# Experts' loop: low halves of the down weights made on GpSimd, those of gate and up on VectorE

## The chip, the cores and the metric

The kernel runs on one core of a Trainium2 chip. The metric is the device time of one execution, in microseconds (us). A core has five instruction streams that meet only at semaphores: TensorE (PE, matmuls; PEld is its weight load), VectorE (DVE), ScalarE (ACT), GpSimd (POOL) and SyncE (SP, which here only issues DMAs). Of these GpSimd also issues the indirect DMAs, the gathers and scatters by a list of row numbers.

## What is computed

The reference is two transformer-like blocks over 1024 tokens of width 1024. The change touches the expert layer, which is computed twice (once in each layer of the second block). Each of 16 experts takes its 128 best tokens, and adds its result to their rows:

```python
def ec_moe(h, w_router, w_gate, w_up, w_down):
    cap = EC_FACTOR * s // N_EXPERTS                 # 128 tokens for each of 16 experts
    aff = jax.nn.softmax(logits, axis=-1)
    gates, idx = lax.top_k(aff.transpose(0, 2, 1), cap)
    xs = jax.vmap(lambda hb, ib: hb[ib])(h, idx)     # gather
    g = jnp.einsum('becd,edf->becf', xs, w_gate)
    u = jnp.einsum('becd,edf->becf', xs, w_up)
    y = jnp.einsum('becf,efd->becd', jax.nn.silu(g) * u, w_down)
    y = y * gates[..., None].astype(y.dtype)
    ...                                              # scatter with add
```

## The kernel before

**Three passes.** A float32 product is made of reduced-precision parts. Each weight matrix `w` is split into a high part (a copy in the reduced type `fp32r`) and a low part (`w` minus the high part), and `three_passes` multiplies high by high, high by low, low by high. So for every weight slot two passes over 128 x 4096 elements are made ahead of the matmuls: the high part by ScalarE (`cast`, L3014) and the low part by VectorE (`low`, L3083). Both inputs of the low pass lie in SBUF.

**The weight ring.** All weights come in slots of 2 MB, through a ring of four buffers (`ring`). SyncE issues the load of slot n+4 when ScalarE has released slot n (L128 waits for L110). Each expert has three slots: gate, up and down. The order in the list is gate 0, up 0, gate 1, up 1, down 0, gate 2, up 2, down 1 and so on, so the down weights of expert e are slot 3e+4. The low part is written over the slot itself (`ring_r` is the same memory under the reduced type), the high part into one of four areas (named `oN_r` and `hT_r` in the trace).

**The loop.** Each engine runs its own loop over the experts, written as turns of four (`per_turn`). I write G, U and D for the gate, up and down products of an expert; each of G, U and D is 24 matmuls of 512 columns. In the iteration of expert j the engines do:

- TensorE: G of j+1, four transposes of the next expert's tokens (`turn_x`), four of the activation `a` (L2992), U of j+1, four more of `turn_x`, then D of j in two halves. D waits for the low part of the down weights.
- ScalarE: cast of slot 3j+4 (down), `gate` (release, SiLU), a copy of the tokens' high part, a copy of a's high part, cast of 3j+5 (gate), release of up, tokens again, cast of 3j+6 (up), and then the two halves of y (L3073), scaled out of PSUM; the second releases the down slot.
- VectorE: low of 3j+4 (down), `low_x` (L3134), low part of a (L3160), low of 3j+5 (gate), `gated` (L3140, silu(g) times u), `low_x`, low of 3j+6 (up).
- GpSimd: when y of e is in SBUF it runs a tiny add that takes the wait (`moe_taker`, 128 x 1, L2901), issues the scatter of e (L2920), runs another taker, and issues the gather of expert e+4 (L2911). Then it waits for the scatter's landing and raises `y_gone`, for which ScalarE waits before it overwrites that y buffer two experts later.

Semaphore `w_split` counts all low parts in the order of the slots; TensorE waits for its count ahead of each product.

Of the kernel before, what the change touches and what calls it, by code (L numbers as in the profile page):

```python
# [6 lines left out]
F32 = mybir.dt.float32  # L7
# [14 lines left out]
RING = 4  # L22
# [346 lines left out]
def start(eng, *sems):  # L369

    for s in sems:
        eng.nop().then_inc(s, 2)
# [2470 lines left out]
def moe_stage(nc, m, layer):  # L2843


    with Stage(nc, f"moe{layer}") as st:
        NE, CAP, EJ, K4 = 16, P, 4, 4
        TURNS = NE // EJ
        first = m["ring"].take(3 * NE)
# [13 lines left out]
        buf, buf_r = m["ring"].buf, m["ring"].buf_r  # L2863
        w_high = [m[t_][:, h_ * NT // 2:(h_ + 1) * NT // 2, :].rearrange("p t n -> p (t n)")
                  for t_ in ("oN_r", "hT_r") for h_ in range(2)]
# [2 lines left out]
        TP, AP_ = st.ps("xt_ps", [P, 4, P]), st.ps("at_ps", [P, 4, P])  # L2868
        G, U, Y = st.ps("g_ps", [P, 2, HALF]), st.ps("u_ps", [P, 2, HALF]), st.ps("y_ps", [P, 2, HALF])
        (wr_in, logits, lt_in, lt_turned, shifted, exped, aff_in, aff_T, work_in, topped, sel_T, sel_in, stepped,  # L2870
         xt_done, xt_cast, xt_in, w_cast, w_split, g_done, u_done, gu_free, sg_in, a_in, at_done, at_cast, at_in,
         y_done, y_in,
         added, y_gone) = (
            st.sem(x) for x in (
                "wr_in", "logits", "lt_in", "lt_turned", "shifted", "exped", "aff_in", "aff_T", "work_in", "topped", "sel_T", "sel_in",
                "stepped", "xt_done", "xt_cast", "xt_in", "w_cast", "w_split", "g_done", "u_done",
                "gu_free", "sg_in", "a_in", "at_done", "at_cast", "at_in", "y_done", "y_in", "added", "y_gone"))
        xs_in = [st.sem(f"xs_in{b}") for b in range(EJ)]
        block = st.block()
# [3 lines left out]
        SLOTS = 3 * EJ  # L2883

        def w_views(n, k):

            high, low = w_high[n % RING], buf_r[:, (first + n) % RING, :]
            return [v.rearrange("p (k n) -> p k n", k=k) for v in (high, low)]
# [6 lines left out]
        @block.gpsimd  # L2895
        def _(pool):
            pool.wait_ge(sel_in, 1)

            def take_wait(n):

                pool.tensor_tensor(taker[:, n:n + 1], zero[:], zero[:], ALU.add)  # L2901

            pool.memset(zero[:], 0.0).then_inc(zeroed, 1)
            pool.wait_ge(zeroed, 1)

            def gather(e):

                if e >= EJ:
                    pool.wait_ge(xt_in, 2 * (e - EJ + 1) + 1)
                take_wait(e)  # L2910
                pool.indirect_dma_start(xs[:, e % EJ, :], None, m["h"], bass.IndirectOffsetOnAxis(ap=rows[:, e:e + 1], axis=0))\  # L2911
                    .then_inc(xs_in[e % EJ], 16)

            start(pool, y_gone)
            for e in range(EJ):
                gather(e)
            for e in range(NE):
                pool.wait_ge(y_in, 2 * (e + 1) + 2)
                take_wait(NE + e)
                pool.indirect_dma_start(m["x1"], bass.IndirectOffsetOnAxis(ap=rows[:, e:e + 1], axis=0), y[:, e % 2, :],  # L2920
                                        None, compute_op=ALU.add).then_inc(added, 16)
                if e + EJ < NE:
                    gather(e + EJ)
                pool.wait_ge(added, 16 * (e + 1))
                pool.nop().then_inc(y_gone, 1)

        @block.tensor
        def _(pe):
# [32 lines left out]

            def product(i, j, what, done, n):

                pe.wait_ge(w_split, i * SLOTS + n + 1)
                if what is G:
                    pe.wait_ge(xt_in, i * (2 * EJ) + 2 * (j + 1) + 1)
                    pe.wait_ge(gu_free, i * EJ + (j + 1))
                w = w_views(n, KD)
                for k in range(KD):
                    ins = three_passes(pe, what[:, j % 2, :], [x_[:, j % 2, k, :] for x_ in (x_high, x_low)],  # L2970
                                       [w_[:, k, :] for w_ in w], k == 0, k == KD - 1)
                ins.then_inc(done, 1)
# [8 lines left out]
            def body(i, more):  # L2981

                for j in range(EJ):
                    nxt, after = more or j + 1 < EJ, more or j + 2 < EJ
                    if nxt:
                        product(i, j + 1, G, g_done, 3 * j + 2)
                    if after:
                        turn_x(i, j + 2, 0)
                    pe.wait_ge(a_in, i * EJ + (j + 1))
                    pe.wait_ge(at_in, i * EJ + (j + 1))  # L2990
                    for k in range(K4):
                        ins = pe.transpose(AP_[:, k, :], a[:, j % 2, k * P:(k + 1) * P], ids[:])  # L2992
                    ins.then_inc(at_done, 1)
                    if nxt:
                        product(i, j + 1, U, u_done, 3 * j + 3)
                    if after:
                        turn_x(i, j + 2, 1)
                    n = 3 * j + 4 if nxt else 3 * j + 2
                    w = w_views(n, K4)
                    pe.wait_ge(w_split, i * SLOTS + n + 1)  # L3000
                    pe.wait_ge(at_in, i * EJ + (j + 2))
                    for half in range(2):
                        pe.wait_ge(y_in, i * (2 * EJ) + 2 * j + half + 1)
                        for k in range(K4):
                            ins = three_passes(pe, Y[:, half, :], [a_[:, j % 2, k, :] for a_ in (a_high, a_low)],
                                               [w_[:, k, half * HALF:(half + 1) * HALF] for w_ in w], k == 0, k == K4 - 1)
                        ins.then_inc(y_done, 1)
# [70 lines left out]
        def _(dve):  # L3078
            step = Steps(dve, stepped)
            def low(i, n):  # L3080
                b = (first + n) % RING
                dve.wait_ge(w_cast, i * SLOTS + n + 1)
                dve.tensor_tensor(buf_r[:, b, :], buf[:, b, :], w_high[n % RING].bitcast(F32), ALU.subtract)\  # L3083
                   .then_inc(w_split, 1)
# [67 lines left out]
            def body(i, more):  # L3152
                for j in range(EJ):
                    nxt, after = more or j + 1 < EJ, more or j + 2 < EJ
                    if nxt:
                        low(i, 3 * j + 4)
                    if after:
                        low_x(i, j + 2, 0)
                    dve.wait_ge(at_cast, i * EJ + (j + 1))
                    dve.tensor_tensor(a_low[:, j % 2, :, :], AP_[:, :, :], a_high[:, j % 2, :, :].bitcast(F32), ALU.subtract)\  # L3160
                       .then_inc(at_in, 1)
                    if nxt:
                        low(i, 3 * j + 5)
                        gated(i, j + 1)
                    if after:
                        low_x(i, j + 2, 1)
                        low(i, 3 * j + 6)
# [219 lines left out]
```

## Time and profile before

| | us |
|---|---|
| three runs | 4507.63, 4508.22, 4508.64 |
| profiled execution, its own time | 4506.89 |
| its span | 4505.1 |
| TensorE busy | 3856.6 (86%) |
| VectorE busy | 2588.6 (57%) |
| GpSimd busy | 502.5 (11%) |
| first expert layer, taker of the first scatter to last write of y | 2934.27 to 3215.16 |
| second expert layer, taker of the first scatter to last write of y | 4186.53 to 4469.89 |

The profiled execution's time is 1.8 us over its span. Times in the rows are counted from the span's start. In a row of the timeline stand: start, duration, engine, line, operation, output and inputs, shapes; in brackets how long the engine was idle just before, and who released it. An instruction that is held back by another engine's use of memory does not show as idle: its row is longer. In a row of the windows stand, for each engine, busy time and number of instructions, then the clock that TensorE was granted (1.00 is 2.4 GHz, 0.50 is 1.2 GHz), the share of time in which the DMA engines were busy, and GB/s.

### The profile page before, as it was taken

What the parts mean: (1) busy time and instruction counts of PE and PEld (TensorE: products, weight loads), DVE (VectorE), ACT (ScalarE), POOL (GpSimd) and SP (SyncE); (2) the same over time, 40 slices, a digit from 0 to 9 for tenths busy, and PEclk for the clock granted to TensorE, in tenths of its full rate; (3) what the DMA queues carried; (4) which work ended last, traced back from release to release, by engine and by line L of the source; (5) the groups of instructions that cost most, each with busy time, mean ns of one, the idle gap of its engine ahead of it and who ended that gap; (6) DMA issues with size and microseconds to landing.
All of it is one profiled execution on the core that took longest, in us unless ns stands there. A gap on an engine that the chain in (4) does not pass through costs nothing. (4 is left out here: it accounts for less than half of the span.)

```text
span 4505.1 us, 56411 instructions
## 1 busy us (share of the span) xinstructions
PE 3856.6 (86%) x22256; PEld 3126.4 (69%) x22256; DVE 2588.6 (57%) x3973; ACT 1651.8 (37%) x2217; POOL 502.5 (11%) x471
## 2 busy tenths in 40 slices
PE   5988998977897999999797999499677798994996
PEld 2766876766676888886697887277566587872774
DVE  6266771159555555555433773587655465745776
ACT  2213331146330000003113773276613465732675
POOL 0001121000000000000131000034102000000341
PEclk9989999989898999999898999699888899996998
DMA  7101112230431111111213103299702302022998
GB/s 296 42 22 61 64 64 96 73 126 22 140 134 66 56 37 56 53 40 69 91 59 142 34 16 137 93 377 371 237 21 81 83 21 110 15 103 94 352 377 277
DMA packets 136489, 518.88 MB, mean 115 GB/s; under 512 B 17952, under 2 KB 70336, under 8 KB 118224
## 3 DMA queue, kind: packets, MB, share of 16 engines
q1 hardware_dynamic: 101936, 411.94, 24.9%
q0 software_dynamic: 31216, 101.85, 7.2%
q8 instruction: 149, 2.44, 0.2%
q10 hardware_dynamic: 3120, 2.10, 0.2%
q14 instruction: 68, 0.56, 0.0%
HBM read 427.21 MB, written 88.62 MB: 115 GB/s over the span
## 5 line engine op out<-in xcount | busy, mean ns | idle before, releaser
L2038 ACT ACTIVATE mlp_relu<-mlp_z 128x512 f32<-128x512 f32 x64 | 38.3, 598 | 641.1 <-PE mlp_z L155 641.1
L3083 DVE TENSOR_TENSOR ring_r<-ring,oN_r 128x4096 fp32r<-128x4096 f32 x48 | 212.2, 4424 | 67.4 <-ACT oN_r L3014 67.4
L153 PE MATMUL scans_G<-ring_r 128*128 128x512 f32 x544 | 221.8, 408 | 32.7 <-ACT scans_stg L2541 18.7
L3083 DVE TENSOR_TENSOR ring_r<-ring,hT_r 128x4096 fp32r<-128x4096 f32 x48 | 212.3, 4423 | 58.0 <-ACT hT_r L3014 58.0
L153 PE MATMUL mlp_z<-ring_r,mlp_w_high_r 128*128 128x512 f32 x512 | 201.3, 393 | 22.0 <-DVE ring_r L147 21.9
L3014 ACT ACTIVATE oN_r<-ring 128x4096 fp32r<-128x4096 f32 x48 | 174.0, 3628 | 84.1 <-DMA ring<-in_w_all 70.0
L154 PE MATMUL mlp_z<-hT_r,mlp_w_high_r 128*128 128x512 f32 x512 | 200.2, 391 | 0.0
L155 PE MATMUL mlp_z<-ring_r 128*128 128x512 f32 x512 | 200.2, 391 | 0.0
L153 PE MATMUL mlp_y_ps<-mlp_w_high_r,oN_r 128*128 128x512 f32 x512 | 199.6, 390 | 0.0
L155 PE MATMUL mlp_y_ps<-mlp_w_high_r,oN_r 128*128 128x512 f32 x512 | 199.2, 389 | 0.0
L154 PE MATMUL mlp_y_ps<-ring_r,oN_r 128*128 128x512 f32 x512 | 199.2, 389 | 0.0
L3014 ACT ACTIVATE hT_r<-ring 128x4096 fp32r<-128x4096 f32 x48 | 174.0, 3630 | 67.5 <-DMA ring<-in_w_all 67.2
L2901 POOL TENSOR_TENSOR moe_taker<-moe_zero 128x1 f32<-128x1 f32 x64 | 144.5, 2258 | 425.9 <-ACT moe_y L3073 413.4
L154 PE MATMUL scans_G<-hT_r,ring_r 128*128 128x512 f32 x480 | 191.6, 399 | 0.0
L155 PE MATMUL scans_G<-ring_r 128*128 128x512 f32 x480 | 191.5, 399 | 0.0
L2096 DVE TENSOR_TENSOR mlp_y<-mlp_y_ps,mlp_gt 128x512 f32<-128x512 f32 x128 | 88.3, 690 | 120.4 <-PE mlp_y_ps L155 118.1
L153 PEld LDWEIGHTS scans_G<-ring_r 128*128 128x128 f32 x544 | 105.0, 193 | 59.4 <-POOL ring_r L2390 14.6
L153 PE MATMUL even_gemm_acc<-even_gemm_w_high,even_gemm_h_high 128*128 128x384 f32 x384 | 133.8, 348 | 13.6 <-DVE ring_r L147 13.6
L2085 DVE TENSOR_TENSOR mlp_relu<-mlp_relu 128x512 f32<-128x512 f32 x64 | 44.2, 691 | 170.7 <-ACT mlp_relu L2038 170.7
L1257 DVE CUSTOM_DVE_ANT_0 even_sc<-even_scores,even_table 128x1024 f32<-128x1024 f32 x96 | 117.0, 1220 | 23.3 <-issue 23.3
L154 PE MATMUL even_gemm_acc<-ring_r,even_gemm_h_high 128*128 128x384 f32 x384 | 130.0, 339 | 0.0
L155 PE MATMUL even_gemm_acc<-even_gemm_w_high,hT_r 128*128 128x384 f32 x384 | 129.7, 338 | 0.0
(643 smaller groups left out, 10661.7 us busy)
## 6 DMA issues: line engine op xcount, KB each, us to landing
ring<-in_w_all SPq DMA_DIRECT2D x118, 2048.0 KB, 10.6
ring<-in_w_mlp SPq DMA_DIRECT2D x16, 2048.0 KB, 7.7
ring<-in_w_all SPq DMA_DIRECT2D x12, 1024.0 KB, 6.3
branch_gates<-scans_stg POOLq DMA_DIRECT2D x48, 256.0 KB, 2.3
merge_raw<-branch_gates SPq DMA_DIRECT2D x16, 768.0 KB, 5.1
ring<-in_w_even SPq DMA_DIRECT2D x6, 1536.0 KB, 8.2
qk_turned<-even_gemm_y POOLq DMA_DIRECT2D x48, 128.0 KB, 2.2
even_qk<-qk_turned SPq DMA_DIRECT2D x6, 1024.0 KB, 5.2
```

The source lines that it names most:

```text
L153: pe.matmul(out, lh, rh, start=start, stop=False)
L154: pe.matmul(out, lh, rl, start=False, stop=False)
L155: return pe.matmul(out, ll, rh, start=False, stop=stop)
L1257: dve.tensor_tensor_reduce(out=sc[:, u % 3, :], in0=SA[:, 2 * (u % 2):2 * (u % 2) + 2, :].rearrange("p a n -> p (a n)"), in1=table[:, c:c ...
L2038: act.activation(r[:, n % 2, :], Z[:, n % 4, :], ACT.Relu).then_inc(z_free, 1)
L2085: step(dve.tensor_tensor(r[:, n % 2, :], r[:, n % 2, :], r[:, n % 2, :], ALU.mult))
L2096: dve.tensor_tensor(y[:, n % 2, :], Y[:, n % 4, :], gt[:, cols], ALU.mult).then_inc(y_free, 1)
L2901: pool.tensor_tensor(taker[:, n:n + 1], zero[:], zero[:], ALU.add)
L3014: act.activation(w_high[n % RING], buf[:, (first + n) % RING, :], ACT.Copy).then_inc(w_cast, 1)
L3083: dve.tensor_tensor(buf_r[:, b, :], buf[:, b, :], w_high[n % RING].bitcast(F32), ALU.subtract)\
```

## The change

In the experts' loop the low pass of the down weights leaves VectorE's program and enters GpSimd's. `low_down(0)` stands behind the first four gathers, `low_down(e+1)` behind the issue of scatter e and of gather e+4 and ahead of the wait for the scatter's landing. It counts a semaphore of its own, `d_split`, and TensorE waits for it ahead of D; `w_split` now counts only gate and up. In VectorE's program the low pass of the gate weights now stands ahead of `gated` and directly behind the low part of `a`, as before, and the iteration begins with `low_x`.

```diff
+            def low_down(e):
+                n = 3 * e + 4 if e + 1 < NE else 3 * NE - 1
+                b = (first + n) % RING
+                pool.wait_ge(w_cast, n + 1)
+                pool.tensor_tensor(buf_r[:, b, :], buf[:, b, :], w_high[n % RING].bitcast(F32), ALU.subtract)\
+                    .then_inc(d_split, 1)
+
             start(pool, y_gone)
             for e in range(EJ):
                 gather(e)
+            low_down(0)
             for e in range(NE):
                 pool.wait_ge(y_in, 2 * (e + 1) + 2)
...
                 if e + EJ < NE:
                     gather(e + EJ)
+                if e + 1 < NE:
+                    low_down(e + 1)
                 pool.wait_ge(added, 16 * (e + 1))
...
-                pe.wait_ge(w_split, i * SLOTS + n + 1)
+                pe.wait_ge(w_split, i * (2 * EJ) + 2 * j + (1 if what is G else 2))
...
-                    pe.wait_ge(w_split, i * SLOTS + n + 1)
+                    pe.wait_ge(d_split, i * EJ + (j + 1))
...
                     nxt, after = more or j + 1 < EJ, more or j + 2 < EJ
-                    if nxt:
-                        low(i, 3 * j + 4)
                     if after:
                         low_x(i, j + 2, 0)
                     dve.wait_ge(at_cast, i * EJ + (j + 1))
                     dve.tensor_tensor(a_low[:, j % 2, :, :], AP_[:, :, :], a_high[:, j % 2, :, :].bitcast(F32), ALU.subtract)\
                        .then_inc(at_in, 1)
+                    if after:
+                        low(i, 3 * j + 5)
                     if nxt:
-                        low(i, 3 * j + 5)
                         gated(i, j + 1)
```

On GpSimd, from the last of the first four gathers (expert 3) to the gather of expert 4, before and after. `moe0_taker` is the tiny add, `x_rows` the target of the scatter, `moe0_xs` that of the gather:

```order
L2911 DMA moe0_xs<-h_rows,moe0_rows 128x1024
L2901 TENSOR_TENSOR moe0_taker<-moe0_zero 128x1
L2920 DMA x_rows<-moe0_y,moe0_rows 1024x1024
L2901 TENSOR_TENSOR moe0_taker<-moe0_zero 128x1
L2911 DMA moe0_xs<-h_rows,moe0_rows 128x1024
```

```order
L2911 DMA moe0_xs<-h_rows,moe0_rows 128x1024
L2918 TENSOR_TENSOR ring_r<-ring,oN_r 128x4096
L2901 TENSOR_TENSOR moe0_taker<-moe0_zero 128x1
L2928 DMA x_rows<-moe0_y,moe0_rows 1024x1024
L2901 TENSOR_TENSOR moe0_taker<-moe0_zero 128x1
L2911 DMA moe0_xs<-h_rows,moe0_rows 128x1024
L2918 TENSOR_TENSOR ring_r<-ring,hT_r 128x4096
```

The two rows `ring_r<-ring,...` are the low passes of the down weights of experts 0 and 1; the second stands behind the first scatter and the gather of expert 4.

On VectorE, the start of the loop's body, expert 0, before and after:

```order
L3083 TENSOR_TENSOR ring_r<-ring,oN_r 128x4096
L3133 ISA
L3134 TENSOR_TENSOR moe_x_low<-moe_xt_ps,moe_x_high 128x512
L3159 ISA
L3160 TENSOR_TENSOR moe_a_low<-moe_at_ps,moe_a_high 128x512
L3082 REGISTER_ALU
L3083 TENSOR_TENSOR ring_r<-ring,oN_r 128x4096
L3138 REGISTER_ALU
L3140 TENSOR_TENSOR moe_a<-moe_sg,moe_u_ps 128x512
```

```order
L3144 TENSOR_TENSOR moe_x_low<-moe_xt_ps,moe_x_high 128x512
L3167 ISA
L3168 TENSOR_TENSOR moe_a_low<-moe_at_ps,moe_a_high 128x512
L3092 ISA
L3093 TENSOR_TENSOR ring_r<-ring,oN_r 128x4096
L3148 REGISTER_ALU
L3150 TENSOR_TENSOR moe_a<-moe_sg,moe_u_ps 128x512
```

The first low pass (down) is gone; the second (gate) keeps its place between the low part of `a` and `gated`. TensorE's and ScalarE's programs keep their order.

## Rows read from the trace of the kernel before

**Rows 1.** Windows: most of the first experts' loop, columns as above
```profile
2934.00:3191.00 257.00, 245.50 (x1098) 191.71 (x1097) 204.60 (x92) 183.14 (x118) 98.25 (x51) 0.99 1.00 371
```

**Rows 2.** Waits of TensorE in that stretch: us in total, times, longest
```profile
PE moe_xt_ps L2959 <- DMA moe_xs<-h_rows,moe_rows: 5.2, 3, 2.7
PE moe_xt_ps L2959 <- DVE moe_x_low L3134: 3.5, 7, 1.0
PE moe_g_ps L153 <- DVE moe_x_low L3134: 2.0, 2, 1.1
```

**Rows 3.** Timeline of one iteration: ScalarE, VectorE and TensorE's first matmul of D
```profile
3013.49 3.63 ACT L3014 ACTIVATE hT_r<-ring 128x4096 fp32r<-128x4096 f32 x1 [2.03 <-DMA ring<-in_w_all]
3017.16 4.42 DVE L3083 TENSOR_TENSOR ring_r<-ring,hT_r 128x4096 fp32r<-128x4096 f32 x1 [2.39 <-ACT hT_r L3014]
...
3022.10 0.68 DVE L3160 TENSOR_TENSOR moe_a_low<-moe_at_ps,moe_a_high 128x512 fp32r<-128x512 f32 x1
3022.70 4.41 DVE L3083 TENSOR_TENSOR ring_r<-ring,oN_r 128x4096 fp32r<-128x4096 f32 x1
3023.02 0.49 PE L153 MATMUL moe_y_ps<-hT_r,moe_a_high 128*128 128x512 f32 x1
3027.03 0.68 DVE L3140 TENSOR_TENSOR moe_a<-moe_sg,moe_u_ps 128x512 f32<-128x512 f32 x1
3027.94 0.69 DVE L3134 TENSOR_TENSOR moe_x_low<-moe_xt_ps,moe_x_high 128x512 fp32r<-128x512 f32 x1 [0.23 <-DVE moe_a L3140]
```

**Rows 4.** Source view of L2390, GpSimd's low pass in the scans stage: ns min/median/max
```profile
L2390 POOL TENSOR_TENSOR ring_r<-ring,ring_r x16: 2350/4604/6728, 294.7 to 737.3; 128x2048 fp32r<-128x2048 f32 x14, 128x1024 fp32r<-128x1024 f32 x2
```

**Rows 5.** Timeline: GpSimd and VectorE at the same time, scans stage and experts' loop
```profile
487.33 4.70 POOL L2390 TENSOR_TENSOR ring_r<-ring,ring_r 128x2048 fp32r<-128x2048 f32 x1 [19.05 <-ACT ring_r L2546]
...
487.66 4.93 DVE L2773 TENSOR_TENSOR scans_E<-scans_c 128x512 f32<-128x512 f32 x1
492.51 0.68 DVE L2774 TENSOR_TENSOR scans_E<-scans_c 128x512 f32<-128x512 f32 x1
...
2978.34 4.42 DVE L3083 TENSOR_TENSOR ring_r<-ring,oN_r 128x4096 fp32r<-128x4096 f32 x1 [2.04 <-ACT oN_r L3014]
...
2978.49 5.14 POOL L2911 DMA_INDIRECT moe_xs<-h_rows,moe_rows  x1 [0.16 <-issue]
```

**Rows 6.** Timeline of GpSimd: taker of the first scatter, and a later expert's four instructions
```profile
2934.27 3.28 POOL L2901 TENSOR_TENSOR moe_taker<-moe_zero 128x1 f32<-128x1 f32 x1 [41.65 <-ACT moe_y L3073]
...
3011.55 3.27 POOL L2901 TENSOR_TENSOR moe_taker<-moe_zero 128x1 f32<-128x1 f32 x1 [12.65 <-ACT moe_y L3073]
3014.97 1.60 POOL L2920 DMA_INDIRECT x_rows<-moe_y,moe_rows  x1 [0.15 <-issue]
3016.03 0.77 POOL L2901 TENSOR_TENSOR moe_taker<-moe_zero 128x1 f32<-128x1 f32 x1
3016.95 0.99 POOL L2911 DMA_INDIRECT moe_xs<-h_rows,moe_rows  x1 [0.16 <-issue]
```

**Rows 7.** Timeline of ScalarE and GpSimd: last y writes, and the second layer's first taker
```profile
3203.53 0.69 ACT L3073 ACTIVATE moe_y<-moe_y_ps,moe_gates 128x512 f32<-128x512 f32 x1 [2.24 <-PE moe_y_ps L155]
3206.34 0.69 ACT L3073 ACTIVATE moe_y<-moe_y_ps,moe_gates 128x512 f32<-128x512 f32 x1 [2.12 <-PE moe_y_ps L155]
...
3214.47 0.69 ACT L3073 ACTIVATE moe_y<-moe_y_ps,moe_gates 128x512 f32<-128x512 f32 x1 [2.13 <-PE moe_y_ps L155]
...
4186.53 2.76 POOL L2901 TENSOR_TENSOR moe_taker<-moe_zero 128x1 f32<-128x1 f32 x1 [41.41 <-ACT moe_y L3073]
...
4469.20 0.69 ACT L3073 ACTIVATE moe_y<-moe_y_ps,moe_gates 128x512 f32<-128x512 f32 x1 [2.12 <-PE moe_y_ps L155]
```

**Rows 8.** DMA view of the first loop: KB each, median us from issue to landing
```profile
ring<-in_w_all SPq DMA_DIRECT2D x39, 2048.0 KB, 10.4
```

**Rows 9.** Around one pause of TensorE: a window of 10 us, and the timeline's row
```profile
3150.00:3160.00 10.00, 7.31 (x31) 5.91 (x30) 7.68 (x2) 7.62 (x7) 6.08 (x4) 0.83 1.02 398
...
3156.00 1.11 PE L2959 MATMUL moe_xt_ps<-identity,moe_xs 128*128 128x128 f32 x4 [2.69 <-DMA moe_xs<-h_rows,moe_rows]
```

More of the change, by code:

```diff
@@ L2870, in moe_stage @@
         (wr_in, logits, lt_in, lt_turned, shifted, exped, aff_in, aff_T, work_in, topped, sel_T, sel_in, stepped,
-         xt_done, xt_cast, xt_in, w_cast, w_split, g_done, u_done, gu_free, sg_in, a_in, at_done, at_cast, at_in,
+         xt_done, xt_cast, xt_in, w_cast, w_split, d_split, g_done, u_done, gu_free, sg_in, a_in, at_done, at_cast, at_in,
          y_done, y_in,
@@ L2875, in moe_stage @@
                 "wr_in", "logits", "lt_in", "lt_turned", "shifted", "exped", "aff_in", "aff_T", "work_in", "topped", "sel_T", "sel_in",
-                "stepped", "xt_done", "xt_cast", "xt_in", "w_cast", "w_split", "g_done", "u_done",
+                "stepped", "xt_done", "xt_cast", "xt_in", "w_cast", "w_split", "d_split", "g_done", "u_done",
                 "gu_free", "sg_in", "a_in", "at_done", "at_cast", "at_in", "y_done", "y_in", "added", "y_gone"))
```

## The prediction

> **What bounds the kernel now.** I read the windows first, to see which engine fills the experts' loop. TensorE is busy 245.5 of 257 us, VectorE 204.6, ScalarE 183.1, GpSimd 98.3, and the DMA engines are busy all the time [rows 1]. Two limits stand side by side, TensorE's own work and the weight loads. VectorE is not one of them: TensorE's waits for it add up to 5.5 us in the first loop [rows 2], so all that a faster VectorE could give is about 11 us in both loops. The timeline of one iteration shows where the moved work stands. ScalarE's cast of the down weights ends at 3017.12, VectorE's low pass runs from 3017.16 to 3021.58, and the first matmul of D stands at 3023.02 [rows 3]. TensorE wants these weights 5.9 us after the cast, and VectorE needs 4.4 of them.
>
> **The moved pass on GpSimd.** The trace has no GpSimd pass of 128 x 4096, but the same operation with the same types in smaller shapes: 2.35 us for 1024 columns and 4.60 for 2048 [rows 4]. A further 1024 cost 2.25 us, so 4096 cost 2.35 + 3 x 2.25 = 9.1 us. From above, twice 4.60 is 9.2; from below, nothing in the trace supports less than VectorE's 4.42. I take 9.1, since the two shapes lie on a line.
>
> The Trainium skill bears on this price: its page "GPSIMD Engine Reference", section "Performance versus the Vector engine", gives the two-input add as 1.96 times slower on GpSimd. By that the pass would take 1.96 x 4.42 = 8.7 us, and the sum below would be some 11 us smaller. The rows of this kernel give 9.1.
>
> **Who holds whom.** GpSimd's pass of 4.70 us started at 487.33, and a VectorE operation of 128 x 512 behind it took 4.93 us where its twin took 0.68: it ended 0.6 us after GpSimd did, so it had done nothing until then. The other way round, an indirect gather of normally 0.99 us took 5.14 us when a VectorE low pass had started 0.15 us ahead of it [rows 5, 6], and GpSimd's taker takes 3.27 us in the loop because a low pass runs beside it. So a two-input pass on VectorE and a pass or an indirect issue on GpSimd exclude each other for the length of an instruction. The two low passes that stay on VectorE (8.8 us an expert) therefore don't run beside the 9.1 us on GpSimd. The operations with one input in PSUM (`low_x`, low part of a, `gated`) I take as free of this.
>
> **The new loop of one expert**, step by step. I write t = 0 for the moment at which the low part of the down weights of one expert is finished and its D may start.
> - VectorE's low pass of the gate weights has been held by GpSimd's pass, since its cast follows that pass's start. It starts at 0. To `gated` 4.33 (3022.70 to 3027.03), to `low_x` 0.91, to the next low pass 0.60 (as 3022.10 to 3022.70), and the low pass of the up weights 4.42 [rows 3]: it ends at 10.26.
> - Meanwhile TensorE runs D. In the last experts, where nothing else holds y, its two halves come 2.81 us apart, and y is in SBUF 2 x 2.81 + 0.1 + 0.69 = 6.4 us after D's start [rows 7]. So y waits for nobody, but GpSimd's taker is held until 10.26.
> - GpSimd: end of taker 0.06, to the scatter 0.15, to the next taker 1.06, to the gather 0.92, gather 0.99 [rows 6]: 3.2 us. At 13.4 the low pass of the next down weights starts. Its cast, which ScalarE begins after y, is over by then: 6.4 + 3.63 = 10.0.
> - The pass itself, 9.1, and 0.1 to hand over.
>
> Sum: 10.26 + 3.2 + 9.1 + 0.1 = 22.6 us an expert. Today y of expert 0 is taken at 2934.27 and that of expert 14 is written at 3207.03 [rows 6, 7], a round of 19.5 us, in which TensorE is busy for 245.5 / 257, that is 18.6, and all loads are done. Both fit into 22.6. The loads have more time than before: gate weights, released at 6.4, land after 10.4 [rows 8] at 16.8 and are cast at 20.4, ahead of 22.6; up weights, released when the next G is done (two products after t = 0, 11.4), are cast by 25.4, 2.8 us into the next round, where 5.8 are to be had.
>
> **TensorE's pause and its clock.** TensorE now pauses some 3.5 us ahead of every D. A pause of 2.69 us was followed by a granted clock of 0.50 (1.2 GHz), and the average of 0.83 over 10 us says for 3.4 us; that costs 1.7 us [rows 9]. Here these 1.7 us make D end later, at 8.1 instead of 6.4 with y. The taker is held until 10.26 anyway, and the casts of gate and up, 1.7 later too, still come in time (22.1 and 4.5), so it costs nothing in the loop. Uncovered it would be 1.7 x 28 = 48 us.
>
> **The sum, first layer.** I take D of expert 0 as unmoved: GpSimd has nothing to do between the gathers and the first y (it is idle for 41.65 us there [rows 6]), and TensorE has G and U of expert 1 to run between the cast and D. The first taker is as now: 2934.27 + 3.28 + 0.15 + 1.06 + 0.92 + 0.99 = 2940.7, and with 9.1 + 0.1 D of expert 1 starts at 2949.9. Eleven rounds of 22.6 lead to expert 12 at 3198.5. The next two have no gather to issue and are 0.92 + 0.99 = 1.9 shorter: 20.7 each, 3239.9 for expert 14. For the last expert there are no low passes on VectorE left, but its own on GpSimd stands behind the scatter of expert 14: 6.4 + 0.1 + 0.2 + 0.15 + 1.06 + 9.1 + 0.1 = 17.1, so D at 3257.0 (today the last y comes 8.1 us behind the one before it, at 3214.47 after 3206.34). With the slow clock after that pause y ends 8.1 later, at 3265.1 against 3215.16: **49.9 us more**. The second layer begins 1252.3 us later with a taker shorter by 0.5: 4516.9 against 4469.89, **47.0 more**. What follows either loop is only shifted. Together 96.9, on the profiled execution's 4506.9: 4603.8; that execution lies 1.3 under the median, so **4605**.
>
> What VectorE saves, 4.42 x 16 x 2 = 141 us, is worth nothing in this, since VectorE stands still behind GpSimd for longer than that. Removing the `w_split` order and adding `d_split` costs a semaphore count on both sides, nothing. On GpSimd's queue the scatter's landing is waited for behind the low pass; it lands meanwhile, and y is written again only two experts later.
>
> **Rivals.**
> - **R1, no exclusion at this place.** If the two engines run side by side, GpSimd's round is 6.4 + 0.2 + 3.2 + 9.1 + 0.1 = 19.0, no more than TensorE's, and loads keep setting the pace. Only the ends of the loops cost: 17.1 for 8.1 at the last expert, 9.0 twice, and a few us at expert 1, whose pass stands behind the first scatter: 4526 to 4535. Against it speak rows 5. 8%.
> - **R2, faster.** The mechanism is TensorE's wait for VectorE: the 11 us would go if the down weights were ready within the 5.9 us between cast and D. It decides at a GpSimd pass of 5.9 us with free memory: 4497. Rows 4 say 9.1. 3%.
> - **R3, the round closes better.** If the taker gets in ahead of VectorE's low pass of the up weights, GpSimd's 3.2 us begin at 6.6 and the low pass falls in behind them only in part. Rounds of 20.5 to 21.5 give 2 us less in 13 rounds of two layers: 4545 to 4570. It needs the cast of the up weights to be late by 3 us. 8%.
> - **R4, a longer round.** Loads that land late (cast of gate or up behind t = 0 or 5.8), or the slow clock on the path where the taker isn't held: up to 1.7 us more in 14 rounds, twice: up to 4655. 12%.
> - **R5, nothing moves.** The GpSimd pass is hidden whole, last expert included, within 9 us of now. 3%.
>
> The skill has a rule that speaks against the change, in "Perfetto Trace Analysis", "Optimizing Scalar/DVE Operations": offloading between VectorE and GpSimd may not help because they share an SBUF port. The trace agrees, as said at rows 5.
>
> **Numbers.** The forecast has 66% (4580 to 4635, by 0.8 us more or less a round). From 4555 to 4655 it holds that, R4 and half of R3, 82%. The measurement can tell 0.2%, 9 us. Faster by more 3%, within 3%, slower 94%.
>
> **What will show it.** The new pass on GpSimd near 9.1 us; VectorE's low passes with a mean near 4.42 for up and near 10 for many of gate (those that are held are long rows); D about 22.6 us apart; TensorE waiting some 2 to 3.5 us for GpSimd ahead of each D, with a granted clock under 0.95 in the loop; the DMA share under 0.95. I am wrong if VectorE's passes keep 4.42 beside GpSimd's (R1), if D follow in 20 us or less, or if another wait than that for the down weights stands ahead of D.

## The result

The changed kernel takes 4613.91 us (median of 4 runs, 4612.09 to 4617.1) beside 4507.93 of the kernel before (4 runs, 4505.3 to 4508.64). The ratio is 1.0237, with a 95% interval of 1.0219 to 1.0255: slower by 2.4%, 106 us. The forecast was 4605. The profiled execution has a span of 4610.3 us against 4505.1, and its 105.2 us more are split nearly evenly: the last scatter of the first expert layer is issued at 3268.70 instead of 3215.61 (53.1 us later), that of the second at 4575.22 instead of 4470.31 (104.9, so 51.8 of its own).

### The profile page after: what moved, and what is told of

The parts are those of the page before. It is cut to its first block and busy times, and to the rows that moved or that the text cites. A ratio compares the mean times of both kernels' runs of the same rounds, so it can differ in the third digit from the quotient of the medians.

```text
span 4610.3 us, 56315 instructions
## 1 busy us (share of the span) xinstructions
PE 3878.3 (84%) x22256; PEld 3151.6 (68%) x22256; DVE 2535.8 (55%) x3941; ACT 1656.4 (36%) x2217; POOL 720.7 (16%) x503
## 5 line engine op out<-in xcount | busy, mean ns | idle before, releaser
L3093 DVE TENSOR_TENSOR ring_r<-ring,oN_r 128x4096 fp32r<-128x4096 f32 x34 | 196.2, 5777 | 71.4 <-ACT oN_r L3024 71.4
L3093 DVE TENSOR_TENSOR ring_r<-ring,hT_r 128x4096 fp32r<-128x4096 f32 x30 | 172.7, 5755 | 48.9 <-ACT hT_r L3024 48.7
L2918 POOL TENSOR_TENSOR ring_r<-ring,hT_r 128x4096 fp32r<-128x4096 f32 x18 | 163.7, 9094 | 2.0 <-ACT hT_r L3024 1.8
L2918 POOL TENSOR_TENSOR ring_r<-ring,oN_r 128x4096 fp32r<-128x4096 f32 x14 | 125.9, 8993 | 49.0 <-ACT oN_r L3024 48.8
```

What stands on the lines that cost most here:

```text
L2918: pool.tensor_tensor(buf_r[:, b, :], buf[:, b, :], w_high[n % RING].bitcast(F32), ALU.subtract)\
```

## The profile after

The windows of both experts' loops, columns as in [rows 1]:

```profile
2934.00:3240.00 306.00, 262.60 (x1138) 208.01 (x1136) 195.61 (x81) 193.59 (x121) 195.70 (x66) 0.95 0.89 325
4220.00:4540.00 320.00, 281.28 (x1220) 224.00 (x1219) 201.55 (x85) 202.10 (x130) 200.41 (x67) 0.95 0.88 321
```

In [rows 1] the DMA share was 1.00 and TensorE was busy 96% of the time. Now the share is 0.89, TensorE is busy 86%, and no engine is full: not VectorE (64%), not GpSimd (64%). A loop in which nothing is full is bound by a chain that goes from engine to engine. TensorE's waits in the first loop (us in total, times, longest) name one link of it; the gathers of [rows 2] are gone from the list:

```profile
PE moe_y_ps L153 <- POOL ring_r L2918: 39.4, 13, 4.6
PE moe_g_ps L153 <- DVE moe_x_low L3144: 0.4, 1, 0.4
```

The moved pass in the source view (ns min/median/max), and VectorE's low passes as groups of the page (busy us, mean ns, idle before them):

```profile
L2918 POOL TENSOR_TENSOR ring_r<-ring,hT_r x18: 8953/8996/9554, 2939.3 to 4555.9; 128x4096 fp32r<-128x4096 f32 x18
...
L3093 DVE TENSOR_TENSOR ring_r<-ring,oN_r 128x4096 fp32r<-128x4096 f32 x34 | 196.2, 5777 | 71.4 <-ACT oN_r L3024 71.4
...
L3093 DVE TENSOR_TENSOR ring_r<-ring,hT_r 128x4096 fp32r<-128x4096 f32 x30 | 172.7, 5755 | 48.9 <-ACT hT_r L3024 48.7
```

GpSimd needs 9.0 us for what VectorE did in 4.42. VectorE has 32 passes fewer, 141 us of work by [rows 3], but its busy time fell only from 2588.6 to 2535.8 us: the 64 passes that stayed have a mean of 5.77 instead of 4.42, and those 86 us are time in which VectorE was held, shown as busy.

**One round**, in the timelines of GpSimd, VectorE, ScalarE and TensorE. The first low pass of GpSimd ends at 3016.05, which is t = 0 in the prediction's notation, and the next starts 13.36 us later:

```profile
3007.11 8.94 POOL L2918 TENSOR_TENSOR ring_r<-ring,oN_r 128x4096 fp32r<-128x4096 f32 x1
3011.55 8.80 DVE L3093 TENSOR_TENSOR ring_r<-ring,oN_r 128x4096 fp32r<-128x4096 f32 x1 [3.99 <-ACT oN_r L3024]
3016.18 0.79 PE L153 MATMUL moe_y_ps<-oN_r,moe_a_high 128*128 128x512 f32 x1 [4.25 <-POOL ring_r L2918]
...
3020.26 0.67 DVE L3150 TENSOR_TENSOR moe_a<-moe_sg,moe_u_ps 128x512 f32<-128x512 f32 x1
...
3021.78 4.42 DVE L3093 TENSOR_TENSOR ring_r<-ring,hT_r 128x4096 fp32r<-128x4096 f32 x1
3024.74 0.69 ACT L3083 ACTIVATE moe_y<-moe_y_ps,moe_gates 128x512 f32<-128x512 f32 x1 [2.26 <-PE moe_y_ps L155]
3025.33 3.62 ACT L3024 ACTIVATE hT_r<-ring 128x4096 fp32r<-128x4096 f32 x1
3025.51 0.73 POOL L2901 TENSOR_TENSOR moe_taker<-moe_zero 128x1 f32<-128x1 f32 x1 [9.46 <-ACT moe_y L3083]
...
3029.41 9.02 POOL L2918 TENSOR_TENSOR ring_r<-ring,hT_r 128x4096 fp32r<-128x4096 f32 x1
```

The second row is the one to learn from. VectorE's pass of the gate weights is issued at 3011.55, waits 4.5 us inside its own row for GpSimd to finish, and then needs 4.3: a row of 8.80 us without idle time before it that would say so. Its successors end at 3026.20, and only then can GpSimd's taker, at 3025.51, get through. Each engine waits for the other once in a round.

The Trainium skill, page "SBUF — State Buffer", section "🔬 SBUF: two separate sides", describes this as a lock on a port pair that whichever instruction starts first keeps for its whole length, for a VectorE operation with two SBUF inputs against a GpSimd operation that reads SBUF. This trace agrees (8.80 against 4.42). The first experiment below has three exceptions to "starts first", if one goes by where the rows open; the last section gives one.

**Every other round is of another kind.** Here the up weights come late, and the pause ahead of D is short:

```profile
3038.48 0.50 PE L153 MATMUL moe_y_ps<-hT_r,moe_a_high 128*128 128x512 f32 x1 [1.36 <-POOL ring_r L2918]
...
3041.16 3.63 ACT L3024 ACTIVATE oN_r<-ring 128x4096 fp32r<-128x4096 f32 x1 [3.36 <-DMA ring<-in_w_all]
3044.82 4.43 DVE L3093 TENSOR_TENSOR ring_r<-ring,oN_r 128x4096 fp32r<-128x4096 f32 x1 [0.58 <-ACT oN_r L3024]
3046.01 3.29 POOL L2901 TENSOR_TENSOR moe_taker<-moe_zero 128x1 f32<-128x1 f32 x1 [7.58 <-ACT moe_y L3083]
3052.43 8.97 POOL L2918 TENSOR_TENSOR ring_r<-ring,hT_r 128x4096 fp32r<-128x4096 f32 x1
```

The cast of the up weights waited 3.36 us for its load and ends at 3044.79. VectorE's pass starts behind it, at 3044.82, and the taker is held until it ends, so the pass stands at 14.0 us behind t = 0 (3038.43). After two rounds of 22.3 us, the pass starts of the first layer are 22.6 to 23.3 and 22.3 us apart in turn; eleven rounds from 2939.26 to 3188.16 give a mean of 22.63.

## Experiments

Each was timed beside the kernel before, whose medians in these batches are 4508 to 4510 us.

### GpSimd works, and nobody waits for it

The kernel before, with two passes on GpSimd over a buffer of their own:

```diff
+                if e + 1 < NE:
+                    for _ in range(2):
+                        pool.tensor_tensor(aside[:], aside[:], aside[:], ALU.subtract).then_inc(beside, 1)
+                        beside_n[0] += 1
+                        pool.wait_ge(beside, beside_n[0])
                 pool.wait_ge(added, 16 * (e + 1))
```

> The kernel before, with all low passes on VectorE, and beside them two GpSimd passes of 128 x 2048 on a buffer of their own (9.2 us an expert, nothing is computed with them), behind the issue of gather e+4. No engine waits for these passes except GpSimd itself. My theory (two-input passes on VectorE and passes on GpSimd exclude each other): three low passes of 4.42 and 9.2 us on GpSimd must be done in turn, 22.5 us, and with GpSimd's indirect issues at least 24.5 us an expert; 5 to 7 us more in 28 rounds, 4650 to 4710. Rival (no exclusion for this pair, R1): 4508, within 10, and VectorE's low passes keep 4.42.

Measured: 4591.64 us, ratio 1.0186 (1.0165 to 1.0206). VectorE's three passes an expert and GpSimd's two now hold each other, in its timelines:

```profile
3040.96 7.67 DVE L3092 TENSOR_TENSOR ring_r<-ring,oN_r 128x4096 fp32r<-128x4096 f32 x1
3048.56 7.82 DVE L3092 TENSOR_TENSOR ring_r<-ring,hT_r 128x4096 fp32r<-128x4096 f32 x1
...
3011.65 1.61 POOL L2924 DMA_INDIRECT x_rows<-moe_y,moe_rows  x1 [0.15 <-issue]
3012.72 4.46 POOL L2902 TENSOR_TENSOR moe_taker<-moe_zero 128x1 f32<-128x1 f32 x1
...
3012.71 4.43 DVE L3092 TENSOR_TENSOR ring_r<-ring,oN_r 128x4096 fp32r<-128x4096 f32 x1
```

The mere use of GpSimd costs 83 us, though nobody waits for its product. What TensorE waits for most is what stands behind it in GpSimd's queue: of 31.8 us of waits between 2934 and 3200, 21.5 are for gathers. Exclusion is shown, with R1's premise false. My expectation was too high by 58 us or more. The round is 22.4 us (scatters at 3034.21 and 3056.58), where I had at least 24.5, and 2.0 of these 2.1 us are the price of the two passes: one that nothing holds takes 3.6 us, where a pass of 128 x 2048 in [rows 4] takes 4.6. My passes aside read one area twice and write plain f32; those of [rows 4] read two areas and write fp32r. Which of the two makes them cheaper is not shown. The run shows one thing more: an indirect issue does not hold VectorE. The last row starts at 3012.71, while the scatter's issue (3011.65 to 3013.26) runs, and takes its plain 4.43; the taker beside it, started 0.01 us later, takes 4.46 for 0.2 us of work.

### Passes of VectorE made short

```diff
-                w = w_views(n, KD)
+                w = [w_views(n, KD)[0]] * 2
...
-                dve.tensor_tensor(buf_r[:, b, :], buf[:, b, :], w_high[n % RING].bitcast(F32), ALU.subtract)\
+                dve.tensor_tensor(buf_r[:, b, 0:8], buf[:, b, 0:8], w_high[n % RING][:, 0:8].bitcast(F32), ALU.subtract)\
```

> The changed kernel, but VectorE's low passes of gate and up cover 8 columns of 4096, and G and U are computed with the high part in place of the low one, so the low part of gate and up is left out. My theory: GpSimd's round is then 6.4 + 0.2 + 3.2 + 9.1 + 0.1 = 19.0, loads set the pace at 19.5, and only the ends of the loops cost: 4525 to 4545. Rival (GpSimd's own chain of 9 us and its issues makes the round, and VectorE's passes beside it don't matter): no change, 4605 to 4615.

Measured: 4561.54 us, ratio 1.0119 (1.0099 to 1.0139). Half of the loss is gone, not the three quarters expected. The rounds are 20.3 us in the middle of the first layer and 21.0 in the second, and a link that I had thought idle is now the last:

```profile
3016.22 1.25 ACT L3083 ACTIVATE moe_y<-moe_y_ps,moe_gates 128x512 f32<-128x512 f32 x2
3018.05 3.63 ACT L3024 ACTIVATE hT_r<-ring 128x4096 fp32r<-128x4096 f32 x1 [0.59 <-DMA ring<-in_w_all]
...
3021.76 9.00 POOL L2918 TENSOR_TENSOR ring_r<-ring,hT_r 128x4096 fp32r<-128x4096 f32 x1 [0.88 <-ACT hT_r L3024]
```

GpSimd, past scatter and gather, stands 0.88 us idle for the cast of the down weights. That cast stands behind y in ScalarE's program, and y behind D, and D behind the pass before: a chain of pass, D, y and cast that doesn't contain VectorE at all. The loads have a part in it: here y also stands behind the cast of the up weights, which had waited 3.4 us for its load, and the cast of the down weights then waits another 0.59 us for its own.

### TensorE kept at work in its pause

```diff
                     pe.wait_ge(at_in, i * EJ + (j + 2))
+                    pe.wait_ge(y_in, i * (2 * EJ) + 2 * j + 1)
+                    for _ in range(9):
+                        pe.matmul(Y[:, 0, :], a_high[:, j % 2, 0, :], a_high[:, j % 2, :, :].rearrange("p k n -> p (k n)"),
+                                  start=True, stop=True)
+                    pe.wait_ge(d_split, i * EJ + (j + 1))
```

> The changed kernel with 9 more matmuls of 512 columns ahead of TensorE's wait for the down weights; they write a PSUM area that D starts anew, and only keep TensorE busy for some 2 us of its pause. My theory: the granted clock stays at 1.00 in the loop, D takes 5.6 in place of up to 7.3 us, but y then waits for GpSimd's taker, which VectorE's low pass of the up weights holds: rounds as before, the ends of the loops 2 us shorter each, 4604 to 4614. Rival (the slow clock after each pause is on the path): 1.7 us less in 28 rounds, near 4566.

Measured: 4609.73 us, ratio 1.0226 (1.0209 to 1.0243). The window of the loop shows a full clock:

```profile
2934.00:3190.00 256.00, 239.67 (x1069) 188.85 (x1068) 175.55 (x69) 163.32 (x106) 169.61 (x60) 0.99 0.89 325
```

The clock is 0.99 for 0.95, and the time 4 us less (4608.72 to 4611.06, against 4612.09 to 4617.1). In the changed kernel the slow clock is covered in the rounds with a gather, whose mean is 22.5 us here. The gain is at the end of the loop: in the first layer the pass starts of experts 12 and 13 are 20.36 us apart instead of 21.80, the last two 17.81 instead of 19.20.

### The last down pass given back to VectorE

```diff
-                if e + 1 < NE:
+                if e + 2 < NE:
                     low_down(e + 1)
...
-                    pe.wait_ge(d_split, i * EJ + (j + 1))
+                    if nxt:
+                        pe.wait_ge(d_split, i * EJ + (j + 1))
+                    else:
+                        pe.wait_ge(w_split, 2 * NE + 1)
```

> The changed kernel, but the low pass of the last expert's down weights is made by VectorE again, which has nothing else to do there. My theory: the last round of each loop falls from 19.2 us to the 8 of before, 4614 - 2 x 11 = 4592. Rival (the end of the loop waits for the last load or for the scatter anyway): within 5 us of 4614.

Measured: 4589.98 us, ratio 1.0182 (1.0165 to 1.0199), 24 us less than the changed kernel. Its last scatters are issued 8.0 us apart, where the changed kernel's are 19.7 apart (3249.01 and 3268.70):

```profile
3257.77 1.57 POOL L2928 DMA_INDIRECT x_rows<-moe_y,moe_rows  x1 [0.15 <-issue]
...
3265.73 1.56 POOL L2928 DMA_INDIRECT x_rows<-moe_y,moe_rows  x1 [0.15 <-issue]
```

So two of the 32 passes carried 24 of the 106 us: the last of each layer, with nothing left to run beside it.

### Half of each down pass on either engine

```diff
-                pool.tensor_tensor(buf_r[:, b, :], buf[:, b, :], w_high[n % RING].bitcast(F32), ALU.subtract)\
+                pool.tensor_tensor(buf_r[:, b, 0:SLOT // 2], buf[:, b, 0:SLOT // 2], w_high[n % RING][:, 0:SLOT // 2].bitcast(F32), ALU.subtract)\
...
+            def low_half(i, n):
+                b = (first + n) % RING
+                dve.wait_ge(w_cast, i * SLOTS + n + 1)
+                dve.tensor_tensor(buf_r[:, b, SLOT // 2:SLOT], buf[:, b, SLOT // 2:SLOT],
+                                  w_high[n % RING][:, SLOT // 2:SLOT].bitcast(F32), ALU.subtract).then_inc(d_half, 1)
```

> The changed kernel, but GpSimd makes only the first 2048 columns of each down low pass and VectorE the other 2048, at the place where the kernel before had the whole. My theory: GpSimd's part of the round shrinks by 4.5 us, 22.6 to 18.1, which is under the 19.5 that the loads allow, so the loads set the pace again; what is left is the last round of each loop, 4.5 us longer than before: 4508 + 9, 4510 to 4525. Rival (any GpSimd pass on the way to D costs its full length, hidden or not): 16 x 2 x 4.6 = 147 us less half of what the change cost, above 4550.

Measured: 4536.06 us, ratio 1.0058 (1.0042 to 1.0073), between the two: better than the rival, 11 us over the top of my range. Thirteen rounds of the first layer, from scatter to scatter, take 20.36 us each. The sum had VectorE's passes begin as soon as GpSimd lets go. In about every second round the up load comes too late for that, here in the longest:

```profile
3036.21 3.63 ACT L3025 ACTIVATE oN_r<-ring 128x4096 fp32r<-128x4096 f32 x1 [4.61 <-DMA ring<-in_w_all]
3039.87 4.42 DVE L3094 TENSOR_TENSOR ring_r<-ring,oN_r 128x4096 fp32r<-128x4096 f32 x1 [3.10 <-ACT oN_r L3025]
3041.06 3.29 POOL L2901 TENSOR_TENSOR moe_taker<-moe_zero 128x1 f32<-128x1 f32 x1 [10.10 <-ACT moe_y L3084]
```

### The gather issued ahead of the wait for y

In the changed kernel, and as a control in the kernel before:

```diff
             for e in range(NE):
+                if e + EJ < NE:
+                    gather(e + EJ)
                 pool.wait_ge(y_in, 2 * (e + 1) + 2)
...
-                if e + EJ < NE:
-                    gather(e + EJ)
```

> The changed kernel with the gather of expert e+4 issued ahead of the wait for y of e, not between the scatter and the low pass. My theory: taker and gather (0.92 + 0.99) leave the way from y to the low pass in 11 rounds of each loop: 4614 - 42 = 4572. Rival (the cast of the down weights, which follows y on ScalarE, then stands last): rounds of 21.5, 4590.

> The kernel before with the gather of expert e+4 issued ahead of the wait for y of e. TensorE waits 9 us for gathers in the two loops, and runs slow for 1.7 us behind each of the longer ones. If these waits are on the path: 4490 to 4500. If the weight loads set the pace (the DMA engines are busy all the time), the same bytes take the same time: 4508, within 5.

The changed kernel with this edit: 4584.31 us, ratio 1.0164 (1.0148 to 1.0179), 30 us less, between the two expectations. Between scatter and pass 1.9 us of gather are gone, and a part is given back. Ten of the fifteen passes in this loop take 9.4 to 9.6 us instead of 9.0. GpSimd's timeline shows one of either kind, each with the scatter ahead of it:

```profile
3047.27 1.59 POOL L2930 DMA_INDIRECT x_rows<-moe_y,moe_rows  x1 [0.15 <-issue]
3048.33 9.55 POOL L2918 TENSOR_TENSOR ring_r<-ring,hT_r 128x4096 fp32r<-128x4096 f32 x1
...
3111.34 1.60 POOL L2930 DMA_INDIRECT x_rows<-moe_y,moe_rows  x1 [0.15 <-issue]
3112.94 9.05 POOL L2918 TENSOR_TENSOR ring_r<-ring,hT_r 128x4096 fp32r<-128x4096 f32 x1
...
3070.82 9.03 POOL L2918 TENSOR_TENSOR ring_r<-ring,oN_r 128x4096 fp32r<-128x4096 f32 x1 [0.99 <-ACT oN_r L3024]
```

The long row begins 1.06 us behind the scatter's, within that one's 1.59, and ends 10.61 behind it; the short one begins 1.60 behind and ends 10.65 behind. So the pass is not slower, its row only opens while the issue still runs, and the two take 10.6 us together. In the changed kernel it is 12.0 us from a scatter's start to the end of the pass (3026.40 to 3038.43). The edit gives 1.4 us a round, not 1.9: over 12 rounds of two layers some 34 us, against the 30 measured. The last row is again a pass that waited for ScalarE's cast behind y.

The control: 4506.22 us, ratio 0.9995 (0.9986 to 1.0004), no change. The waits for gathers of [rows 2] are gone, others have grown in their place, and the window still has the loads at full share:

```profile
PE moe_g_ps L153 <- DVE moe_x_low L3134: 6.0, 8, 1.7
...
2934.00:3191.00 257.00, 244.44 (x1099) 190.80 (x1098) 203.90 (x91) 181.74 (x116) 69.01 (x48) 1.00 1.00 368
```

So before the change it was the loads, at 19.5 us an expert, that set the pace; TensorE's small waits moved about within it and were worth nothing. That speaks against R2 as well: if TensorE's waits in this loop, 10.7 us before and 12.0 here, move about without a change of the time, a faster pass would hardly have brought its 11 us. No run made the pass faster than VectorE's.

### Three edits together

The short passes of VectorE, the gather first, and the last down pass on VectorE, in the changed kernel:

> The changed kernel with three edits together: VectorE's low passes of gate and up cover 8 columns only (G and U take the high part for the low one, so these two products leave their low part out), the gather is issued ahead of the wait for y, and the low pass of the last down weights is VectorE's. If the three shares are the whole loss, GpSimd's own chain is y at 6.4 after D's start, taker 0.8, 0.15, to the pass 1.06, pass 9.55, 0.1: 18.2 us, under the loads' 19.5 us a round. What is left is then expert 1 (its pass behind the first scatter) and single late casts: 4515 to 4528. Rival: the cast of the down weights, which stands behind y on ScalarE, still sets the round as in the kernel with short passes alone (20.35 us a round, 4561.5); then only the end and part of the gather come off: 4538 to 4548.

Measured: 4540.44 us, ratio 1.0075 (1.0058 to 1.0092): the rival. Without VectorE, gather or last expert in the way, rounds are still (3125.07 - 2979.50) / 7 = 20.8 us in the middle of the first layer, and 20.6 and 20.5 over thirteen rounds of either. The timeline shows the chain of pass, D, y and cast closed, with GpSimd waiting for the cast and TensorE for the pass:

```profile
3029.83 0.50 PE L153 MATMUL moe_y_ps<-hT_r,moe_a_high 128*128 128x512 f32 x1 [1.93 <-POOL ring_r L2918]
...
3037.39 0.69 ACT L3086 ACTIVATE moe_y<-moe_y_ps,moe_gates 128x512 f32<-128x512 f32 x1 [2.12 <-PE moe_y_ps L155]
3037.97 3.62 ACT L3027 ACTIVATE hT_r<-ring 128x4096 fp32r<-128x4096 f32 x1
...
3041.67 9.03 POOL L2918 TENSOR_TENSOR ring_r<-ring,hT_r 128x4096 fp32r<-128x4096 f32 x1 [1.58 <-ACT hT_r L3027]
```

D and y take from 3029.83 to 3038.08, 8.25 us; the cast is over at 3041.59; the pass ends at 3050.70. That is 20.9 us, over the loads' 19.5. In this chain the slow clock is not covered: the windows of 3031 to 3033 show 0.50, and D with y is 6.7 in the rounds at full clock.

The very next round is of another kind. TensorE's pause ahead of D is 0.99 us and the clock stays at 1.00, but ScalarE waits for loads:

```profile
3053.01 3.63 ACT L3027 ACTIVATE oN_r<-ring 128x4096 fp32r<-128x4096 f32 x1 [2.32 <-DMA ring<-in_w_all]
3056.54 1.24 ACT L3086 ACTIVATE moe_y<-moe_y_ps,moe_gates 128x512 f32<-128x512 f32 x2
3058.68 3.63 ACT L3027 ACTIVATE oN_r<-ring 128x4096 fp32r<-128x4096 f32 x1 [0.90 <-DMA ring<-in_w_all]
```

The cast of the up weights has waited 2.32 us for its load and holds y behind it, and the cast of the down weights waits another 0.90 for its own: 20.7 us. I count the 28 rounds of both layers from the end of one pass to the end of the next. The slow clock lengthens 7 of them (20.9 to 22.1 us), a wait of the down cast for its load 15 (20.1 to 22.1), and the 6 that have neither take 19.3 to 19.6. So the closed chain alone is no longer than the loads' 19.5; what is over comes from the clock in some rounds and from late loads in more.

### The clock in that chain

The same with the nine matmuls in TensorE's pause:

> The kernel with the three edits together, and nine more matmuls in TensorE's pause ahead of D besides (they write the first half of y's PSUM area, which D starts afresh). As there, VectorE's low passes of gate and up cover 8 columns only, so G and U leave their low part out. The three edits left rounds of 20.8 us, made of the pass 9.0, D and both halves of y 8.2, the cast of the next down weights 3.6. Of those 8.2, 1.7 are the slow clock after the pause. Theory: with that chain as the bound the clock is on the path; at full clock it is 19.2 us and the loads' 19.5 take over: 1.3 us x 11 rounds x 2 layers, 29 us less than 4540: 4510 to 4520. Rival: the cast waits for something else (the load of the up weights, whose cast stands ahead of y), and the clock is covered as it was in the changed kernel: 4535 to 4542.

Measured: 4532.41 us, ratio 1.0045 (1.0031 to 1.0059). Eight us less, where 20 to 30 were expected, and the window tells why the test is blunt:

```profile
2934.00:3200.00 266.00, 265.53 (x1221) 214.86 (x1220) 46.31 (x78) 184.72 (x119) 153.50 (x61) 1.00 0.97 358
```

The clock is 1.00, but TensorE is busy for 265.53 of 266 us. A round is 20.3 us (ten rounds from 2980.97 to 3183.76), and TensorE has no pause left in it: the nine matmuls take 2.3 us of it. So my own addition became a bound. The rival's mechanism is there as well: in every one of the 28 rounds the cast of the up weights stands directly ahead of y, and nearly always it has waited some 2.3 us for its load. About 8 us net for the clock fit the 7 long rounds of the kernel ahead, but the intervals of the two ratios just touch; how much the clock would give without the added matmuls is left open.

### Half each, with the gather first

The best two edits that keep the whole computation:

> The changed kernel with half of each down pass on GpSimd and half on VectorE, and the gather issued ahead of the wait for y. Half each alone gave 4536 with rounds of 20.36 us. If the gather's issue (1.9 us between scatter and pass) is on the path, rounds fall to 19.5, where the loads set the pace, 0.85 us x 14 x 2 = 24 us less: 4512 to 4520. Rival: the late cast of the up weights holds the chain, and the gather is hidden: 4530 to 4540. Neither is under the kernel before (4508).

Measured: 4532.96 us, ratio 1.0055 (1.0039 to 1.0072), 3 us under half each alone: the rival. GpSimd's half passes are now held by VectorE's (median 6.57 us instead of 4.62 for `hT_r`), and the cast of the up weights is late here too: in most rounds it starts 3 to 6 us behind D. Which of the two takes the freed 1.9 us was not separated; the profiled execution is also 11 us over the median. Nothing tried beats the kernel before.

## Where the prediction was right, and where a size was off

- **Price of the pass.** 9.1 us by the line through two shapes; measured 9.0. The factor of 1.96 from the Trainium skill, worked out in the prediction, would have given 8.7; measured it is 2.04. The row decides, and the difference is small.
- **Exclusion.** Right, and shown by the kernel with passes aside. The operations with an input in PSUM are free of it, as assumed: `low_x` and the low part of `a` take 0.69 and 0.68 at 3031.46 and 3032.07, within GpSimd's pass of 3029.41 to 3038.43. Said too widely was that an indirect issue excludes a pass of VectorE: it is held by one, but does not hold one. No term of the sum hung on that.
- **The round.** 22.6 predicted, 22.63 and 22.64 measured. In the round shown, VectorE's chain ends at 10.15 (10.26 predicted) and the pass starts at 13.36 (13.4). That the mean hits as well is luck in part: I had the up weights cast 2.8 us into the round, and in every other round they are at 6.4 (3044.79), which makes 23.1; the other kind, 22.3, is shorter since its first part and the pass are each 0.1 shorter than summed.
- **The clock.** Covered, as said. But it is not 1.7 us in every round: after a pause of 4.25 us D starts at 0.50 and stays there for 5.4 us, after one of 1.36 us it is not slow at all (1.00 from 3038 on). In the windows of the changed kernel, columns as before:

```profile
3014.50:3015.00 0.50, 0.00 (x0) 0.00 (x0) 0.50 (x1) 0.00 (x0) 0.50 (x1) 1.00 1.01 311
3015.00:3015.50 0.50, 0.00 (x0) 0.00 (x0) 0.50 (x1) 0.00 (x0) 0.50 (x1) 0.54 1.46 606
...
3021.00:3021.50 0.50, 0.50 (x3) 0.37 (x2) 0.33 (x1) 0.50 (x1) 0.00 (x0) 0.50 0.10 41
3021.50:3022.00 0.50, 0.50 (x3) 0.41 (x2) 0.50 (x2) 0.32 (x2) 0.00 (x0) 0.63 0.00 0
```

- **The step that was thin: "Its cast, which ScalarE begins after y, is over by then: 6.4 + 3.63 = 10.0."** With the slow clock y ends at 9.4, and the cast at 12.9 (3028.95), 0.5 us ahead of GpSimd's pass (3029.41). I had checked the 1.7 us of the clock against the taker and the casts of gate and up, and not against this cast. In the round it made no difference; in the first of the two rounds without a gather it did, in both layers. There the pass of 3209.96 waited 0.99 us for the cast and started 12.9 behind its t = 0, where the sum had GpSimd ready at 11.5; with nine matmuls in the pause it waited for none. This cast is also where the short passes and the three edits fell short of what was expected, by the clock in some rounds and by late loads in others.
- **The last rounds: the term that was mis-sized.** 17.1 was predicted for the last one, 19.0 and 20.3 measured. Here nothing covers the slow clock, as these rows of the changed kernel show:

```profile
3240.44 0.80 PE L153 MATMUL moe_y_ps<-hT_r,moe_a_high 128*128 128x512 f32 x1 [3.76 <-POOL ring_r L2918]
...
3240.00:3250.00 10.00, 7.78 (x28) 6.05 (x28) 0.69 (x1) 1.86 (x3) 1.57 (x3) 0.83 0.05 11
...
3249.01 1.56 POOL L2928 DMA_INDIRECT x_rows<-moe_y,moe_rows  x1
3250.04 9.38 POOL L2918 TENSOR_TENSOR ring_r<-ring,hT_r 128x4096 fp32r<-128x4096 f32 x1
...
3267.59 0.69 ACT L3083 ACTIVATE moe_y<-moe_y_ps,moe_gates 128x512 f32<-128x512 f32 x1 [2.13 <-PE moe_y_ps L155]
```

  I put the slow clock into the last D alone. The D before it pauses too: its y is 8.16 us behind its start (3240.44 to 3248.60), not 6.4. The pass's row, directly behind the scatter's, is 9.38 long, since it opens while the issue still runs.
- **The account of the first layer**, measured minus predicted: D of expert 1 at 2948.3 instead of 2949.9 and eleven rounds at 22.63, together -1.3 at expert 12; then +1.2 (the cast), +0.7 (a row of 9.55 that opens within the scatter's), +1.9 (the last round), +0.7 (the last D). That is +3.2, and the last y ends at 3268.3 instead of 3265.1. In the second layer it is +4.8, most of it in the same places (its last round is +3.2). Together 8 of the 9 us between 4605 and 4613.9.
- **The rivals.** R1 and R5 fell with the pass itself and the exclusion. R3 didn't occur in its own form: where the cast of the up weights is late by 3 us, VectorE's pass still starts 1.2 us ahead of the taker (3044.82 against 3046.01), because the taker waits for y, and y stands behind the same cast. Its condition thus defeats itself. R4 is what happens in every other round, with 0.5 us more than summed, so the measured time lies between the forecast and R4.
- **What VectorE was relieved of** is worth nothing, as said; the control shows the stronger reason, which I gave only as one of two: the loads set the pace.

Of the 106 us, then: VectorE's passes carry 52 (short passes). That edit takes away their own time together with the hold on GpSimd, but TensorE waited for VectorE only 0.4 us in the first loop, so it is nearly all the hold. Gather and last expert together carry 21 once that is gone, though alone they gave 30 and 24: the shares overlap and don't add. Some 32 stay with the chain of pass, D, y and cast: by the slow clock, of which full clock gave back 8, and by loads that land late for ScalarE's casts. The two were not separated further.

## What to carry to other kernels

Before a pass is moved from VectorE to GpSimd, look at what its new queue waits for and who is waited for behind it: here one chain went pass, D, y, issue, pass, and a second, pass, D, y, cast, pass, hidden within half a microsecond of it in the round shown. Two engines that exclude each other cannot be added up as capacity; a kernel in which VectorE is busy 80% and is waited for 5 us in 257 had nothing to win from help while the loads set its pace. When a sum has a term "is over by then", put the worst clock into it and write down the margin: once the other chain is shortened by more than that, this one can stand last (the pass of 3070.82 in the gather-first kernel, 0.99 us).

## What the runs showed of the hardware

- The next GpSimd instruction's row can open 1.06 us behind the start of a scatter's issue that takes 1.6. A pass there reads as 9.55 us, where it costs 9.0 behind the issue's end. The sum of an issue and what follows is to be taken from the ends.
- An indirect issue on GpSimd is held by a two-input pass of VectorE ([rows 5]), but does not hold one (4.43 us beside a scatter's issue).
- Which of two such instructions goes first is not always to be read from where the rows open. In the kernel with passes aside a VectorE pass opens at 2968.41, within a gather's issue, and GpSimd's pass at 2969.04. GpSimd's takes its plain 3.62 us, and VectorE's 8.54.
- A GpSimd subtraction of 128 x 2048 takes 3.6 us when both inputs are the same area and the output is f32, and 4.6 from two areas into fp32r.
- A held instruction stands in the trace as a long one. The page counts it as busy; only its duration against an undisturbed twin shows the wait.
